# A second spare buffer for up weights, earlier loads of the second quad's gates, and a compact copy of the sample rows, in a one-core hybrid decoder step

## The chip, the cores and the metric

The kernel runs on one core of a Trainium2 chip. The metric is device time in microseconds (us), the median of three runs.

## The reference, cut to what matters

One inference step for 256 prompt tokens and 32 sample tokens (8 sequences of 4) at model width 1024, all in float32. A pooling mixer and a gated linear-attention mixer are merged, multiplied by `w_out` and added to `x`. Then comes a routed mixture of 32 experts, and a last norm:

```python
x = x + einsum(merged, w_out)
h = rmsnorm(x, norm2_w)
# group top-1 of 4, expert top-2 of 8, weights combine[token, expert]
act = silu(h @ w_gate[e]) * (h @ w_up[e]) * combine[..., e]
x = x + sum_e act @ w_down[e]        # w_gate, w_up: 1024 x 256, w_down: 256 x 1024
y = rmsnorm(x, final_norm_w)
```

The weights of one expert are three matrices of 1 MB each, so the mixture reads 96 MB.

## The kernel before, in words

**Stages.** Input projection, mixers, branch products, output product, mixture, final norm. The change touches the output product and the mixture, which fill the span from about 329 us to its end.

**Output product** (PE `wo_half` L1868, DVE `step_evac` L2778). It runs in nine steps, `WO_STEPS`: step 0 makes the 32 sample rows, steps 1 to 4 and 5 to 8 make the two prompt tiles, 256 output columns per step. Step 1 + j and step 5 + j read the j-th buffer of `w_out`. These four buffers are slots 2, 3, 4, 5. The semaphore `wo_pe` counts the finished steps, `wo_dve` the steps that DVE (L2782) has added to `x2`. The sample rows lie in `x2s` with 128 partitions by 256 columns: partition 32 g + token holds columns 256 g onwards. After each step POOL multiplies the new rows by the norm weights (`n2b`, `n2bs`) into `x2p` (prompt, L889) or `x2d` (sample, L881). `x2d` is 128 by 1024, block diagonal: for each chunk k of 128 features it holds a 128 by 128 matrix in which only the four 32 by 32 blocks on the diagonal aren't zero. POOL clears all of it first (L874) and writes the blocks in four linked instructions. ACT scales `x2p` and `x2d` by the row norms (L1207).

**Gather.** `G` holds for each token tile a 128 by 128 matrix of zeros and ones that says which token sits in which of 128 seats: 4 experts (a "quad") times 32 seats. PE gathers the rows of a quad with one product per chunk k and token tile t, `src[:, k, :]` against `G[:, t, :]`, all 128 by 128: in `gathers` (L1927) for the first quad, 8 chunks by 3 tiles, and in `gather_next` (L2019) for each next one, 24 products in a row. A float32 product shows as two matmul records in the trace.

**Quads.** There are 8 quads of 4 experts. For quad q PE runs (`quad_products`, L2092) gate products, up products (L2013, 32 products each, in tiles of 128 by 32), two flips, the gather for quad q + 1 (L2025), the down products (L2068) and `way_back` (L2088, L2085), which spreads the result to the tokens. The last two quads are ordered otherwise (`last_pair`): gate(6), gather, up(6), gate(7), down(6), up(7), down(7).

**Loads.** All weight loads are issued in a fixed order by SP (L582, L591), each 1 MB into one slot; a load waits until the slot's last reader is done, and all that is behind it in the queue waits too. Gates go to slots 8, 9, 11, 12 (`EVEN_GATES`) or 2, 3, 4, 5 (`ODD_GATES`), ups to 13, 14, 15, 6 (`UPS`), downs to 7, 10, 0, 1. SP's order around the change:

1. gates, ups and downs of quad 0;
2. gates of quad 1 into slots 2 to 5, each after `item_read` of the slot's last user, which for a buffer of `w_out` is `wo_pe` >= 9, the end of all steps (L407);
3. after the last logits (`lgt` >= 3) one up weight of quad 1 into a spare slot (`SPARE`, slot 16, in the room of `h2T`);
4. gates of quad 2 in eight half loads (`gates_in_parts` L585), four of them when PE is half through the gate products of quad 0 (`m_gate0`), four after all of them (`m_gate`);
5. the other three ups of quad 1 after `m_up` >= 1;
6. downs of quad 1 after `m_dn1` >= 1, the end of quad 0's down products; gates of quad 3 after `m_gate` >= 2; ups of quad 2 after `m_up` >= 2; downs of quad 2 after `m_dn1` >= 2, and so on.

The final norm's weights are loaded by ACT's queue (L1169, L1171) after quad 1, into the room of `n2b`.

```python
held, v = item_read(reader_ahead(A_ITEMS, s))   # L630
sp.wait_ge(held, v)
part_load(1, w_gate, QE + e, s)
...
sp.wait_ge(S["m_dn1"], q)                       # L610
for e, s in enumerate(DOWNS):
    part_load(q, w_down, first + e, s)
```

Of the kernel before, what the change touches and what calls it, by code (L numbers as in the profile page):

```python
# [12 lines left out]
P = 128  # L13
# [102 lines left out]
SPARE, EARLY = N_SLOTS, UPS[0]  # L116
# [13 lines left out]
def hybrid_step(nc, x_prompt, x_sample, cache_pool, cache_conv, state_delta, norm1_w, w_in, w_pool,  # L130
# [24 lines left out]
    with ExitStack() as ctx:  # L155
# [3 lines left out]
        def sem(name):  # L159
            return ctx.enter_context(nc.semaphore(name))  # L160
# [159 lines left out]
        n2b = b.take(D)  # L320
        n2bs = b.take(D // 4)
        rows_w = b.take(2 * T).rearrange("p (k t) -> p k t", k=2)
        rows_c = b.take(2 * T).rearrange("p (k t) -> p k t", k=2).bitcast(I32)
# [9 lines left out]
        x2d = b.take(D).rearrange("p (k q) -> p k q", k=KD)  # L333
        h2T = b.take(KD * T).rearrange("p (k t) -> p k t", k=KD)
        back1 = b.take(T)
        assert b.at <= b_end, (b.at, b_end)
        slots.append(h2T.rearrange("p k t -> p (k t)")[:, 0:SLOT])
# [56 lines left out]
        ring_in = [sem(f"ring_in{i}") for i in range(N_SLOTS + 1)]  # L394


        def item_read(i):
# [8 lines left out]
            return S["wo_pe"], len(WO_STEPS)  # L406
# [56 lines left out]
        def _(sp):  # L463
# [138 lines left out]
            def ups(q, first):  # L602
                sp.wait_ge(S["m_up"], q)
                for e, s in enumerate(UPS):
                    if s != EARLY or not (isinstance(q, int) and q == 1):
                        part_load(q, w_up, first + e, s)
# [27 lines left out]
            part_load(1, w_up, QE, SPARE)  # L634
# [33 lines left out]
        def _(pool):  # L668
# [205 lines left out]
            link(nc.gpsimd.memset(x2d, 0.0))  # L874
            pool.wait_ge(S["nb_in"], 16 * 5)
            for n, (t, j) in enumerate(WO_STEPS):
                pool.wait_ge(S["wo_dve"], n + 1)
                if t == 2:
                    for g in range(4):
                        own = slice(TS * g, TS * g + TS)  # L880
                        ins = nc.gpsimd.tensor_tensor(x2d[own, :, own], x2s[own, :].rearrange("p (q k) -> p k q", k=KD),  # L881
                                                      n2bs[own, :].rearrange("p (q k) -> p k q", k=KD), ALU.mult)
                        if g < 3:
                            link(ins)
                    ins.then_inc(S["xp_pool"], 1)
                    pool.wait_ge(S["xp_pool"], 1)
# [15 lines left out]
        def _(act):  # L902
# [376 lines left out]
            for i in range(PEEL):  # L1279
                for u in range(2):  # L1280
                    quad_acts(i, u)
                if i == 0:
                    act.wait_ge(S["xp_pool"], len(WO_STEPS))
                    norm_rows(fnb, fnbs, final_norm_w, "nb_in")
# [24 lines left out]
        def _(pe):  # L1309
# [616 lines left out]

            def gathers(t, first=False, last_tile=False):  # L1927

                src = x2d if t == 2 else x2p[:, t]
                for k in range(KD):  # L1930
                    ins = mm(ps[k // 4][:, P * (k % 4):P * (k % 4) + P], src[:, k, :], G[:, t, :],
# [1101 lines left out]
```

## Time and profile before

| what | value |
|---|---|
| median of three runs | 602.62 us (601.82 to 602.76) |
| the profiled execution | 602.27 us |
| its span | 600.5 us |
| PE busy | 548.7 us (91%) |
| PE weight load busy | 409.4 us (68%) |
| DVE, ACT, POOL busy | 45%, 25%, 23% |
| moved by DMA | 158.59 MB, mean 264 GB/s |

The shares are means over stages with different limits: PE's 91% comes from the first 425 us, the DMA engines are full in the last 200. The span is the profiled stretch; the 1.8 us between it and the execution's time lie around it.

### The profile page before, as it was taken

The numbers are of one execution on the slowest core, as the hardware profiler recorded it, in microseconds if no ns is written. First come the engines' busy times: TensorE is split into PE (matmuls) and PEld (weight loads), VectorE is DVE, ScalarE is ACT, GpSimd is POOL, SyncE is SP. The second block draws the span as 40 slices with busy tenths as digits, with TensorE's granted clock in tenths as the row PEclk, the third lists the DMA queues.
The fourth block names the chain that finished last, engine by engine and source line by source line (L and its number), as shares of the span: only waits on it lengthen the run. The fifth ranks groups of instructions, "written<-read, shape, count | busy, mean of one in ns | idle before, by whom it ended". The sixth has DMA issues, their size and how long they took to land.

```text
span 600.5 us, 12000 instructions
## 1 busy us (share of the span) xinstructions
PE 548.7 (91%) x4820; PEld 409.4 (68%) x4820; DVE 270.1 (45%) x754; ACT 147.2 (25%) x389; POOL 135.2 (23%) x228
## 2 busy tenths in 40 slices
PE   8999999999999999999999999999495959699873
PEld 7899999777877755578889888755262626266431
DVE  4567767755443426146546244651314040414125
ACT  3366465237720002033100133111010101010012
POOL 5777774121200540035004421200000000000000
PEclk9999999999999999999999999999789898999988
DMA  9755444839934273542378944999999999999982
GB/s 242 232 159 151 154 142 141 281 112 332 306 87 134 45 264 110 172 123 89 109 260 350 381 180 199 365 422 420 409 422 419 423 420 419 422 420 419 421 330 79
DMA packets 82582, 158.59 MB, mean 264 GB/s; under 512 B 11245, under 2 KB 65274, under 8 KB 70849
## 3 DMA queue, kind: packets, MB, share of 16 engines
q1 hardware_dynamic: 79724, 154.22, 70.1%
q10 hardware_dynamic: 2805, 3.62, 2.0%
q8 instruction: 38, 0.62, 0.4%
q14 instruction: 15, 0.12, 0.1%
HBM read 150.05 MB, written 7.96 MB: 263 GB/s over the span
## 4 chain that ended last, share of the span: by engine, by line
PE 72%; DMA 23%; DVE 2%; SPq 1%; issue 1%; ACT 1%; DVEq 0%; ACTq 0%
DMA arena<-in_w_up_dram 21%; PE ps L1360 21%; PE ps L1369 13%; PE ps L2013 8%; PE ps L1881 5%; PE ps L1830 3%; PE ps L1784 3%; PE ps L1313 2%; DMA arena<-in_w_in_dram 1%; SPq L582 1%; PE ps L1823 1%; PE ps L2088 1%; PE ps L2068 1%; PE ps L1566 1%; PE ps L1530 1%; PE ps L2025 1%
## 5 line engine op out<-in xcount | busy, mean ns | idle before, releaser
L1360 PE MATMUL ps<-arena 128*128 128x288 f32 x480 | 130.1, 416 | 1.2 <-DMA arena<-in_w_in_dram 1.2
L1360 PEld LDWEIGHTS ps<-arena 128*128 128x128 f32 x480 | 87.3, 190 | 26.8 <-issue 3.1
L2013 PE MATMUL ps<-arena 128*32 128x256 f32 x1024 | 69.3, 433 | 29.0 <-DMA arena<-in_w_up_dram 27.6
L2013 PEld LDWEIGHTS ps<-arena 128*32 128x32 f32 x1024 | 40.1, 124 | 56.7 <-issue 43.2
L1369 PE MATMUL ps<-arena 128*128 128x144 f32 x616 | 78.3, 288 | 0.0
L1369 PEld LDWEIGHTS ps<-arena 128*128 128x128 f32 x616 | 76.3, 190 | 2.5 <-issue 1.9
L2229 DVE SCALAR_TENSOR_TENSOR ps<-arena,ps 128x312 f32<-128x312 f32 x72 | 39.1, 545 | 2.4 <-ACT ps L1021 0.9
L2025 PE MATMUL ps<-arena 128*128 128x128 f32 x336 | 38.7, 276 | 0.0
L2025 PEld LDWEIGHTS ps<-arena 128*128 128x128 f32 x336 | 38.1, 192 | 0.4 <-DVE arena L2898 0.4
L2919 DVE TENSOR_TENSOR arena<-arena,ps 128x256 f32<-128x256 f32 x8 | 3.4, 421 | 66.8 <-issue 36.6
L2088 PE MATMUL ps<-arena 128*128 128x512 f32 x64 | 31.2, 618 | 1.9 <-ACT arena L1258 1.0
L1313 PE MATMUL ps<-arena 128*128 128x128 f32 (+7 forms) x162 | 26.5, 282 | 5.8 <-DVE arena L2919 4.7
L1881 PE MATMUL ps<-arena 128*128 128x256 f32 x128 | 31.0, 385 | 0.0
L2068 PE MATMUL ps<-arena 128*32 128x512 f32 x256 | 29.3, 596 | 1.7 <-DMA arena<-in_w_down_dram 1.2
L2935 DVE TENSOR_TENSOR arena<-arena,ps 128x512 f32<-128x512 f32 (+1 forms) x40 | 24.7, 633 | 13.7 <-PE ps L2088 13.7
L1313 PEld LDWEIGHTS ps<-arena 128*128 128x128 f32 (+7 forms) x162 | 19.0, 148 | 12.7 <-issue 5.6
L2088 PEld LDWEIGHTS ps<-arena 128*128 128x128 f32 x64 | 10.3, 189 | 23.0 <-issue 13.8
L2926 DVE COPY arena<-ps 128x512 f32<-128x512 f32 x8 | 5.5, 692 | 44.4 <-PE ps L2068 44.4
L1881 PEld LDWEIGHTS ps<-arena 128*128 128x128 f32 x128 | 23.1, 190 | 2.9 <-issue 0.4
L1252 ACT ACTIVATE arena<-ps 128x256 f32<-128x256 f32 x8 | 3.1, 383 | 82.0 <-PE ps L1313 82.0
L1830 PE MATMUL ps<-arena 128*128 128x144 f32 x168 | 21.0, 287 | 0.1
L1830 PEld LDWEIGHTS ps<-arena 128*128 128x128 f32 x168 | 20.8, 190 | 0.4 <-DVE arena L2741 0.3
(410 smaller groups left out, 747.3 us busy)
## 6 DMA issues: line engine op xcount, KB each, us to landing
arena<-in_w_up_dram SPq DMA_DIRECT2D x32, 1024.0 KB, 17.3
arena<-in_w_gate_dram SPq DMA_DIRECT2D x28, 1024.0 KB, 18.1
arena<-in_w_down_dram SPq DMA_DIRECT2D x28, 1024.0 KB, 18.6
arena<-in_w_in_dram SPq DMA_DIRECT2D x26, 1024.0 KB, 6.7
out_dram<-arena SPq DMA_DIRECT2D x9, 512.0 KB, 7.6
arena<-in_w_branch_delta_dram SPq DMA_DIRECT2D x4, 1024.0 KB, 6.3
arena<-in_w_out_dram SPq DMA_DIRECT2D x4, 1024.0 KB, 5.4
arena<-in_w_gate_dram SPq DMA_DIRECT2D x8, 512.0 KB, 9.5
```

What stands on the lines that cost most here:

```text
L1313: return nc.tensor.transpose(out, in_, ident[0:m, 0:m])
L1360: last = mm(ps[n % 2][:, 0:T], w[:, k, P * (n % 2):P * (n % 2) + P], hT[:, k, :], start=(k == 0), stop=(k == KD - 1))
L1369: last = mm(to[:, 0:HT], left[:, k, :], right[:, k, :], start=(first and k == 0), stop=(k == HK - 1), skip_group_check=True)
L1784: last = mm(ps[BP_BANK[d]][:, 0:T], w[:, k, P * (d % 4):P * (d % 4) + P], ypT[:, k, :], start=(k == 0), stop=(k == NG - 1))
L1830: last = mm(bank[:, 0:HT], left[:, k, :], right[:, k, :], start=(first and k == 0), stop=(k == HK - 1), skip_group_check=True)
L1881: last = mm(bank[:, 0:256], merged[:, k, P * t:P * t + P], w[:, k, :], start=(k == 0), stop=(k == KD - 1))
L2013: last = mm(to[CAP * e:CAP * e + CAP, 0:FE], xgT[u][:, k, CAP * e:CAP * e + CAP], w[e][:, k, :], start=(k == 0), stop=(k == KD - 1))
L2025: last = mm(ps[k // 4][:, P * (k % 4):P * (k % 4) + P], src[:, k, :], G[:, t, :], start=(t == ORDER[0]), stop=(t == ORDER[-1]))
L2068: last = mm(ps[5 + half][CAP * e:CAP * e + CAP, :], actT[u][:, c, CAP * e:CAP * e + CAP], w[:, c, 512 * half:512 * half + 512], start=(c = ...
L2088: last = mm(bank[:, :], back[:, P * t:P * t + P], dn[:, 512 * half:512 * half + 512], start=True, stop=True)
L2229: ins = V.scalar_tensor_tensor(c, e[:, j:j + NACC], smallT[:, NQKV * j + n:NQKV * j + n + 1], c, ALU.mult, ALU.add)
L2935: V.tensor_tensor(v, v, bank[:, 0:v.shape[1]], ALU.add).then_inc(S["m_yadd"], 1)
```

## The change

- `item_read` lets the j-th buffer of `w_out` go at `wo_pe` >= 6 + j, its own last step, in place of 9 for all.
- A second spare slot (17, `spare2`) takes a second up weight of quad 1. It lies where `n2b` and `n2bs` are, so SP waits for `xp_pool` >= 9, POOL's last product, before it loads there. Slot 14 joins slot 13 in `EARLY`: no load goes to it for quad 1. Both spares share a semaphore, on which PE waits for 32.
- ACT waits for `m_up` >= 2 before it loads the final norm's weights into `n2b`.
- To make room, `x2d` shrinks from 1024 to 256 columns: 128 partitions by 8 chunks by 32. The clearing of it is gone, and POOL writes it in one instruction. The four row copies `rows_c`, `rows_w` go to four separate rooms.
- The gather product of the sample tile becomes four products for each chunk, each 32 rows by 32 columns of stationary data (`src[own, k, :]`) against 32 rows by 128 of `G`, into its own 32 partitions of the bank. `gather_next` takes the tiles in the order 0, 2, 1 (before: 2, 0, 1).

```diff
@@ -113,7 +113,7 @@
 UPS, DOWNS = (13, 14, 15, 6), (7, 10, 0, 1)
 LAST_DOWNS = EVEN_GATES
 N_SLOTS = 16
-SPARE, EARLY = N_SLOTS, UPS[0]
+SPARES, EARLY = (N_SLOTS, N_SLOTS + 1), UPS[0:2]
 
 
 WO_STEPS = [(2, None)] + [(t, j) for t in range(2) for j in range(WO_ITEMS)]
@@ -317,10 +317,10 @@
         x2 = b.take(2 * D).rearrange("p (n d) -> p n d", n=2)
         x2s = b.take(D // 4)
         slots.append(b.take(SLOT))
-        n2b = b.take(D)
-        n2bs = b.take(D // 4)
-        rows_w = b.take(2 * T).rearrange("p (k t) -> p k t", k=2)
-        rows_c = b.take(2 * T).rearrange("p (k t) -> p k t", k=2).bitcast(I32)
+        spare2 = b.take(SLOT)
+        n2b = spare2[:, 0:D]
+        n2bs = spare2[:, D:D + D // 4]
+        row_rooms = [b.take(T)]
         assert b.at <= qk_at + NQKV * T
         fnb, fnbs = n2b, n2bs
         b = Cut(qk_at + NQKV * T)
@@ -330,11 +330,15 @@
         assert b.at <= work0 and len(slots) == N_SLOTS
         b = Cut(work0)
         x2p = b.take(2 * D).rearrange("p (n k q) -> p n k q", n=2, k=KD)
-        x2d = b.take(D).rearrange("p (k q) -> p k q", k=KD)
+        x2d = b.take(D // 4).rearrange("p (k q) -> p k q", k=KD)
+        row_rooms += [b.take(T), b.take(T)]
         h2T = b.take(KD * T).rearrange("p (k t) -> p k t", k=KD)
+        row_rooms.append(arena[:, b.at - KD * T + SLOT:b.at - KD * T + SLOT + T])
+        b.take(max(0, SLOT + T - KD * T))
         back1 = b.take(T)
         assert b.at <= b_end, (b.at, b_end)
-        slots.append(h2T.rearrange("p k t -> p (k t)")[:, 0:SLOT])
+        rows_c, rows_w = [v.bitcast(I32) for v in row_rooms[0:2]], row_rooms[2:4]
+        slots.extend((h2T.rearrange("p k t -> p (k t)")[:, 0:SLOT], spare2))
         b = Cut(b_end)
         xgT_room = b.take(2 * KD * P)
         xgT = [xgT_room[:, KD * P * j:KD * P * (j + 1)].rearrange("p (k t) -> p k t", k=KD) for j in range(2)]
@@ -392,6 +396,7 @@
 
         S = Sems()
         ring_in = [sem(f"ring_in{i}") for i in range(N_SLOTS + 1)]
+        ring_in.append(ring_in[SPARES[0]])
 
 
         def item_read(i):
@@ -403,7 +408,7 @@
             i -= BP_ITEMS
             if i < BD_ITEMS:
                 return S["bd_pe"], delta_product(i, P4) if i in BD_FAST else 2
-            return S["wo_pe"], len(WO_STEPS)
+            return S["wo_pe"], len(WO_STEPS) - WO_ITEMS + i - BD_ITEMS + 1
 
 
         free = [0] * N_PROJ
@@ -602,7 +607,7 @@
             def ups(q, first):
                 sp.wait_ge(S["m_up"], q)
                 for e, s in enumerate(UPS):
-                    if s != EARLY or not (isinstance(q, int) and q == 1):
+                    if s not in EARLY or not (isinstance(q, int) and q == 1):
                         part_load(q, w_up, first + e, s)
 
             def ups_downs(q, first):
@@ -631,7 +636,9 @@
                 sp.wait_ge(held, v)
                 part_load(1, w_gate, QE + e, s)
             sp.wait_ge(S["lgt"], NT)
-            part_load(1, w_up, QE, SPARE)
+            part_load(1, w_up, QE, SPARES[0])
+            sp.wait_ge(S["xp_pool"], len(WO_STEPS))
+            part_load(1, w_up, QE + 1, SPARES[1])
 
             def pair_loads(i, ahead):
                 first, then = (i % (QUADS // 2)) * (2 * QE), (ahead % (QUADS // 2)) * (2 * QE)
@@ -871,19 +878,12 @@
             sum_delta_weights(2)
             pool.wait_ge(S["y_done"], N_Y)
             sum_delta_weights(3)
-            link(nc.gpsimd.memset(x2d, 0.0))
             pool.wait_ge(S["nb_in"], 16 * 5)
             for n, (t, j) in enumerate(WO_STEPS):
                 pool.wait_ge(S["wo_dve"], n + 1)
                 if t == 2:
-                    for g in range(4):
-                        own = slice(TS * g, TS * g + TS)
-                        ins = nc.gpsimd.tensor_tensor(x2d[own, :, own], x2s[own, :].rearrange("p (q k) -> p k q", k=KD),
-                                                      n2bs[own, :].rearrange("p (q k) -> p k q", k=KD), ALU.mult)
-                        if g < 3:
-                            link(ins)
-                    ins.then_inc(S["xp_pool"], 1)
-                    pool.wait_ge(S["xp_pool"], 1)
+                    nc.gpsimd.tensor_tensor(x2d, x2s.rearrange("p (q k) -> p k q", k=KD),
+                                            n2bs.rearrange("p (q k) -> p k q", k=KD), ALU.mult).then_inc(S["xp_pool"], 1)
                 else:
                     cols = slice(256 * j, 256 * j + 256)
                     nc.gpsimd.tensor_tensor(x2p[:, t, :, TS * j:TS * j + TS], x2[:, t, cols].rearrange("p (q k) -> p k q", k=KD),
@@ -1281,6 +1281,7 @@
                     quad_acts(i, u)
                 if i == 0:
                     act.wait_ge(S["xp_pool"], len(WO_STEPS))
+                    act.wait_ge(S["m_up"], 2)
                     norm_rows(fnb, fnbs, final_norm_w, "nb_in")
             act.wait_ge(S["route"], 1)
             end = act.value_load(more_i[0:1, 0:1], min_val=0, max_val=MORE_MAX) + QUADS // 2
@@ -1924,12 +1925,16 @@
                         last = mm(bank[at:at + m, 0:NE], strU[0:m, 0:m], picks[0:m, t, :], start=(not before), stop=True)
                     last.then_inc(S["ranked"], 1)
 
+            def tile_rows(t):
+                return [slice(TS * g, TS * g + TS) for g in range(4)] if t == 2 else [slice(0, P)]
+
             def gathers(t, first=False, last_tile=False):
 
                 src = x2d if t == 2 else x2p[:, t]
                 for k in range(KD):
-                    ins = mm(ps[k // 4][:, P * (k % 4):P * (k % 4) + P], src[:, k, :], G[:, t, :],
-                             start=(first and k % 4 == 0), stop=(last_tile and k % 4 == 3), skip_group_check=True)
+                    for own in tile_rows(t):
+                        ins = mm(ps[k // 4][own, P * (k % 4):P * (k % 4) + P], src[own, k, :], G[own, t, :],
+                                 start=(first and k % 4 == 0), stop=(last_tile and k % 4 == 3), skip_group_check=True)
                     if last_tile and k % 4 == 3:
                         ins.then_inc(S[f"m_g{k // 4}"], 1)
 
@@ -1995,10 +2000,10 @@
                 n = i + 1 if table in (EVEN_GATES, ODD_GATES) else 2 * i + u + 1
                 for s in table:
                     base = loads_in(s) if s < RA else 0
-                    if s == SPARE:
-                        pe.wait_ge(ring_in[s], 16)
+                    if s in SPARES:
+                        pe.wait_ge(ring_in[s], 16 * len(SPARES))
                         continue
-                    if s == EARLY and not (isinstance(n, int) and n == 1):
+                    if s in EARLY and not (isinstance(n, int) and n == 1):
                         base = -1
                     if s in EVEN_GATES and not (isinstance(n, int) and n == 1):
                         base = 1
@@ -2020,10 +2025,11 @@
 
                 pe.wait_ge(S["m_G"], q + (NT + 1))
                 for k in range(KD):
-                    for t in ORDER:
+                    for t in (0, 2, 1):
                         src = x2d if t == 2 else x2p[:, t]
-                        last = mm(ps[k // 4][:, P * (k % 4):P * (k % 4) + P], src[:, k, :], G[:, t, :],
-                                  start=(t == ORDER[0]), stop=(t == ORDER[-1]))
+                        for own in tile_rows(t):
+                            last = mm(ps[k // 4][own, P * (k % 4):P * (k % 4) + P], src[own, k, :], G[own, t, :],
+                                      start=(t == 0), stop=(t == 1), skip_group_check=True)
                     if k % 4 == 3:
                         last.then_inc(S[f"m_g{k // 4}"], 1)
 
@@ -2048,7 +2054,7 @@
 
                 q = 2 * i + u
                 wait_from(S["m_act"], q)
-                ups = (SPARE,) + UPS[1:] if isinstance(q, int) and q == 1 else UPS
+                ups = SPARES + UPS[2:] if isinstance(q, int) and q == 1 else UPS
                 loaded(ups, i, u)
                 products(i, u, ups, ps[3]).then_inc(S["m_up"], 1)
...
```

## Rows read from the trace of the kernel before

**Rows 1.** The page: GB/s by slice of 15 us; the chain by line
```profile
GB/s 242 232 159 151 154 142 141 281 112 332 306 87 134 45 264 110 172 123 89 109 260 350 381 180 199 365 422 420 409 422 419 423 420 419 422 420 419 421 330 79
...
DMA arena<-in_w_up_dram 21%; PE ps L1360 21%; PE ps L1369 13%; PE ps L2013 8%; PE ps L1881 5%; PE ps L1830 3%; PE ps L1784 3%; PE ps L1313 2%; DMA arena<-in_w_in_dram 1%; SPq L582 1%; PE ps L1823 1%; PE ps L2088 1%; PE ps L2068 1%; PE ps L1566 1%; PE ps L1530 1%; PE ps L2025 1%
```

**Rows 2.** SP's waits: us, times, longest us
```profile
SPq L582 <- PE ps L1881: 32.5, 1, 32.5
```

**Rows 3.** Timeline of SP's queue, 366 to 409 us
```profile
366.74 1.97 SPq L582 DMA_DIRECT2D arena<-in_w_gate_dram  x4
368.92 0.33 SPq L582 DMA_DIRECT2D arena<-in_w_up_dram  x1
378.51 5.17 SPq L591 DMA_DIRECT2D arena<-in_w_gate_dram  x8
383.73 2.06 SPq L582 DMA_DIRECT2D arena<-in_w_up_dram  x3
396.89 1.75 SPq L582 DMA_DIRECT2D arena<-in_w_down_dram  x4
404.73 1.75 SPq L582 DMA_DIRECT2D arena<-in_w_gate_dram  x4
408.18 1.75 SPq L582 DMA_DIRECT2D arena<-in_w_up_dram  x4
```

**Rows 4.** Busy time by stretch; at the end PEclk, DMA share, GB/s
```profile
354.00:366.00 12.00, 12.00 (x65) 10.62 (x65) 5.18 (x25) 3.81 (x11) 3.34 (x3) 1.00 0.00 0
366.00:378.50 12.50, 11.64 (x113) 9.92 (x115) 8.14 (x38) 5.33 (x9) 2.43 (x6) 1.00 0.86 344
366.00:400.00 34.00, 33.14 (x315) 23.85 (x314) 18.23 (x57) 7.30 (x13) 4.80 (x13) 1.00 0.95 369
402.00:580.00 178.00, 143.63 (x1472) 83.32 (x1464) 49.20 (x118) 12.15 (x25) 0.00 (x0) 0.91 1.01 418
```

**Rows 5.** Timeline of DVE, 353 us
```profile
353.77 0.42 DVE L2782 SCALAR_TENSOR_TENSOR arena<-ps,arena 128x256 f32<-128x256 f32 x1 [1.20 <-PE ps L1881]
```

**Rows 6.** Timeline of POOL, 333 us
```profile
333.13 4.66 POOL L881 TENSOR_TENSOR arena<-arena 32x256 f32<-32x256 f32 x4 [11.60 <-DVE arena L2782]
```

**Rows 7.** Timeline of PE, 366 to 375 and 384 to 402 us
```profile
368.72 2.03 PE L1931 MATMUL ps<-arena 128*128 128x128 f32 x16
371.30 0.41 PE L1924 MATMUL ps<-late_room 128*128 128x32 f32 x2 [0.55 <-DVE late_room L2817]
...
387.74 5.52 PE L2025 MATMUL ps<-arena 128*128 128x128 f32 x48
393.19 3.64 PE L2068 MATMUL ps<-arena 128*32 128x512 f32 x32
```

**Rows 8.** Chain of waits: start us, us, what
```profile
106.26 3.88 PE ps L1360 x16
...
159.32 3.63 PE ps L1566 x128
```

**Rows 9.** Timeline of PE around one L1554 insertion, 190 to 196 us
```profile
190.74 0.75 PE L1360 MATMUL ps<-arena 128*128 128x288 f32 x2
...
194.81 0.64 PE L1554 MATMUL ps<-arena 32*32 32x128 f32 x16
195.38 0.51 PE L1360 MATMUL ps<-arena 128*128 128x288 f32 x1
```

**Rows 10.** Timeline of PE and SP, the last two quads
```profile
547.86 5.63 PE L2025 MATMUL ps<-arena 128*128 128x128 f32 x48
...
554.34 3.66 PE L2013 MATMUL ps<-arena 128*32 128x256 f32 x64 [0.86 <-DMA arena<-in_w_up_dram]
...
558.28 1.90 SPq L582 DMA_DIRECT2D arena<-in_w_up_dram  x4
...
574.52 5.35 PE L2013 MATMUL ps<-arena 128*32 128x256 f32 x64 [2.21 <-DMA arena<-in_w_up_dram]
```

**Rows 11.** Busy time by stretch: the last up products
```profile
575.00:578.50 3.50, 3.50 (x41) 2.23 (x37) 0.00 (x0) 0.00 (x0) 0.00 (x0) 0.54 1.06 390
```

More of the change, by code:

```diff
@@ L2901, in way_back @@
             def way_back(turns):
-                V.scalar_tensor_tensor(back, rows_c[:, 0, :], place[:, 0:1], rows_w[:, 0, :], ALU.is_equal, ALU.mult).then_inc(S["turns"], 1)
-                V.scalar_tensor_tensor(back1, rows_c[:, 1, :], place[:, 0:1], rows_w[:, 1, :], ALU.is_equal, ALU.mult).then_inc(S["turns"], 1)
+                V.scalar_tensor_tensor(back, rows_c[0], place[:, 0:1], rows_w[0], ALU.is_equal, ALU.mult).then_inc(S["turns"], 1)
+                V.scalar_tensor_tensor(back1, rows_c[1], place[:, 0:1], rows_w[1], ALU.is_equal, ALU.mult).then_inc(S["turns"], 1)
                 dve.wait_ge(S["turns"], turns + 2)
@@ L2942, in quad_acts @@
                         dve.wait_ge(S["rows_pe"], k + 1)
-                        V.tensor_copy((rows_c if k < 2 else rows_w)[:, k % 2, :], ps[ROW_BANK[k]][:, 0:T]).then_inc(S["rows_ev"], 1)
+                        V.tensor_copy((rows_c if k < 2 else rows_w)[k % 2], ps[ROW_BANK[k]][:, 0:T]).then_inc(S["rows_ev"], 1)
                     dve.wait_ge(S["rows_ev"], 4)
```

## The prediction

> **What bounds the kernel now.** I read the page first, then SP's waits, then stretches of the DMA engines. In every slice from 390 to 570 us the DMA engines move 409 to 423 GB/s, and the chain that ended last runs for 21% of the span through up loads [rows 1]. From 402 to 580 us the mean is 418 GB/s at a DMA share of 1.01 [rows 4]: the mixture's weights come as fast as they can, one load of 1 MiB (1.049 MB) each 2.51 us. So the end is set by when that unbroken stream begins and by how much it has to carry.
>
> Before it there is a hole. SP waits 32.5 us for the end of the output product [rows 2], and from 354 to 366 us nothing is moved [rows 4]. The change fills this hole with the four gates of quad 1, and adds a load behind them. The question is whether work put into the hole shortens the stream, or only opens a second hole later. For that the order of SP's issues is to be read [rows 3]: four gates at 366.74, one up at 368.92, eight half loads of gates from 378.51, three ups from 383.73, four downs from 396.89. That is 12 MiB, 12.58 MB, ahead of the downs. From 366 to 400 us the engines move 34 us x 369 GB/s = 12.55 MB [rows 4]. So the twelve loads are through at 400.1 us, and the downs, issued 3.2 us earlier, find the engines still busy. The stream has no gap at 396.89, but the queue is only 3.2 us deep there.
>
> **The hole after the change.** The loads of quad 1's gates wait for steps 6, 7, 8 and 9. DVE's addition of the sixth step begins at 353.77 [rows 5], so the first goes then and the last at 366.74 as before; both spares follow at about 369 us. These loads are through by 366.74 + 1.5 + 3 x 2.51 = 375.8 us. (The 1.5 us are the start of an idle queue: from 366 to 378.5 us the engines move 12.5 x 344 = 4.30 MB [rows 4], which is 10.3 us of work at 418 GB/s, so it began in effect at 368.2.) Then the engines stand idle until the half loads at 378.51. Behind those come only two ups in place of three: 6 MiB, 15.1 us from 380.0, through at 395.1. Half loads ran slower before, which the mean of 369 holds; if two more microseconds go there it is 397. In either case the queue is empty when the downs are issued, and their issue waits for PE to finish the down products of quad 0. That semaphore, not the buffers, becomes the bound. If it comes at the same time, the downs start to flow at 396.89 + 1.5 = 398.4 in place of 400.1. **The most that the earlier loads and the spare can give is therefore 1.7 us**, not the 2.5 us of a load, nor the ten of four. What is late next is PE.
>
> **Did PE get slower before that semaphore?** The chain from 372 us is PE nearly without gaps. `gather_next` for quad 1 takes 48 records from 387.74, and the down products start at 393.19, right behind it [rows 7]: 5.45 us, 0.227 us for each full product of two records. Whatever is added to this gather delays the downs by as much. Per chunk the change takes out one full product and puts in four of 32 by 32, eight records, between two full products. The nearest rows for this are the sample tiles L1554: 32 by 32 tiles, 128 columns, each in its own 32 partitions of one bank, sixteen records between full products of L1360. Without them sixteen L1360 records take 3.88 us [rows 8]. With them, the next sixteen start at 190.74, the tiles at 194.81 (4.07 us, 0.19 more), and L1360 goes on at 195.38 (0.57 us) [rows 9]. The insertion costs 0.76 us. Four narrow tiles of 128 columns side by side run at 3.63 us for 128 records [rows 8], 28.4 ns a record, so 0.45 us of it are the records and 0.31 us the way into the narrow tiles and back.
>
> Per chunk then: 8 x 28.4 ns + 0.31 = 0.53 us in place of 0.227, that is +0.31 us, and 8 chunks make **+2.4 us in `gather_next`**. The lower bound is that the switch costs nothing here, 8 x (0.227 - 0.227) = 0. The upper one takes the tiles at the pace inside the insertion, 0.57/16 = 35.6 ns, beside the 0.31 us: 8 x (0.595 - 0.227) = 2.9 us, and 4 us if loads of full weights behind a tile take another 0.13 us a chunk (half of a full product's time, rounded up). I take 2.4, since L1554 is the same shape in the same order.
>
> The Trainium skill says in TensorEngine Tiling (Array Packing), Key Properties, that changing the tiling mode drains TensorE. By that rule a compact tile between full ones isn't free; without the rule one would put this gather at no loss and the change at 1.7 us faster. The trace agrees with the rule, by the 0.31 us worked out above.
>
> **The first gathers.** The sample tile's gather starts at 368.72 and takes 16 records, and PE then waits for DVE until 371.30 [rows 7]. After: 64 x 28.4 ns + 0.31 = 2.1 us, done at 370.9. The cover is 0.4 us; at 35.6 ns a record it would be 371.3, still even. Cost nothing.
>
> **Edits that I cost at nothing.** POOL's four instructions of the sample step, 4.66 us together [rows 6], become one and the clearing goes; PE doesn't wait for POOL there (from 354 to 366 us it is busy 12.00 of 12 us [rows 4]), since DVE's addition and the `w_out` products go on without it, so nothing is won. ACT's scaling of `x2d` shrinks under the same cover. The row copies keep their sizes. SP's wait for `xp_pool` comes no later than the logits' (POOL multiplies while PE makes them), and behind it stand only the half loads of 378.51. ACT's wait for `m_up` >= 2 stands after quad 1's down evacuation, by when it is long met. PE's wait on both spares is at quad 1's ups, after 401 us; both have landed by 378.
>
> **Do the later issues hold?** All after the first gather move by 2.4 us, those after the second by 4.9. Gates of quad 3, 404.73 [rows 3], become 407.2; the downs then flow until 398.4 + 2.4 + 10.0 = 410.8, so 2.1 us of the 3.6 are left after the 1.5 us of a start. Ups of quad 2, 408.18, have a further 10 us. In the last quads the gather of 547.86 ends 2.4 us later, the ups after it start at about 556.2 in place of 554.34, and SP's ups of 558.28 go at 560.1, while the downs ahead of them flow until about 564 [rows 10]. The stream holds.
>
> **Sum.** Earlier loads and spare -1.7, gather +2.4: +0.7 us on the profiled execution's 602.27, so 603.0. That execution lay 0.35 us below the median of the runs, 602.62; I give 603.3 for the median. A measurement of this kernel can tell about 0.2%, 1.2 us, from no change, so this is **no difference**.
>
> **The rivals.**
>
> *The switch hides (faster).* Weight loads of the next tiles run beside the current products and the gather stays at 5.5 us. Then the full 1.7 us come out, 600.9. For it: weight loads lie under products almost everywhere. Against: the insertion's 0.76 us.
>
> *The clock stays up at the end (still no difference).* The last up products run from 574.52 for 5.35 us where the ones at 554.34 took 3.66 [rows 10], at a granted clock of 0.54 of 2.4 GHz, so mostly at 1.2 GHz [rows 11], after a wait of 2.2 us for the load. PE is busier before it after the change, as the gather moves everything behind it. If the clock stays at 2.4 GHz, the tail loses 1.7 us: 601.6.
>
> *The row groups take turns (slower).* At one place, the eight tile records of a chunk, each takes a full record's 0.114 us because the four tiles write one bank: 8 x (0.91 + 0.31 - 0.227) = 7.9 us, less 1.7: 608.8. It decides from a tile record of 60 ns on (8 x (0.48 + 0.31 - 0.227) = 4.5, 605.4). Against: sixteen such records took 0.57 us, not 1.8.
>
> The Trainium skill gives a rule of this kind in TensorEngine Tiling (Array Packing), Gotcha 1: different row tiles can't access the same PSUM bank at once. The trace speaks against it at that same place, L1554.
>
> *The switch costs more than there (slower).* A gather of +4 us, the upper bound above, gives 602.6 + 4.0 - 1.7 = 604.9. From +2.9 us on it could be told from no change.
>
> *The change doesn't do what it says:* an early wait that I think is met, such as `xp_pool`, holds the half loads. It would have to come after 378.51, ten microseconds late. 1 in 100.
>
> **How the numbers follow.** Forecast, gather +1.6 to +3.2 us: 0.5. Switch hidden or nearly: 0.2. Clock stays up: 0.08. Gather +3.2 to +5: 0.16. Turns, wholly or in part: 0.05. The rest 0.01. With a gather of +2.9 and more the time is past 603.8, so 0.08 of the forecast's 0.5 count as slower. Same: 0.42 + 0.07 of the clock's 0.08 = 0.49. Faster: 0.2 + 0.01 = 0.21. Slower: 0.08 + 0.16 + 0.05 + 0.01 = 0.30. The range runs from the hidden switch, 600.9 or 0.2 less, to a gather of +4: 600.7 to 605.0. What is left out is the turns and a part of either end.
>
> **What would show it.** In the profile after: SP issues single gate loads from 353.8 us; a DMA hole from about 376 to 380 us and one from about 396 to 400; the L2025 group at quad 0 with 96 records over 7.9 us; the downs of quad 1 issued at 399.3 with an idle queue, the first landing some 5 us later; 418 GB/s from there. I am wrong on the gather if it takes under 6.5 or over 9 us, and wrong on the stream if a hole comes after 402 us or if the downs still find a busy queue.

## The result and the profile after

The changed kernel takes **605.33 us** (median of 4 runs, 605.16 to 605.61) against 602.34 for the kernel before: ratio 1.0052, 95% interval 1.0033 to 1.0071, 3 us slower. I had forecast 603.3 and no difference, and a range up to 605.0. The profiled execution took 605.44 us, its span is 603.7, PE is busy 563.3 us of it (548.7 before) with 5204 matmul records (4820). The 384 more records are the narrow products: in each of eight gathers, eight chunks with eight narrow records for two full ones.

The page of the changed kernel, part 2, in slices of 15.1 us (before: [rows 1]):

```profile
GB/s 239 233 159 150 153 141 141 280 115 327 282 109 132 56 251 116 164 132 79 115 252 348 403 279 290 282 296 423 407 421 418 421 419 422 421 419 422 348 368 79
```

The slices at 347 and 362 us show the plan of the change: 180 and 199 GB/s before, where the output product ends, and 279 and 290 now. The slice at 377 us has fallen from 365 to 282: the gap between the early loads and the half loads, which was expected. But the slice at 392 us has gone from 422 to 296 and the one at 558 us from 421 to 348: two places where the full stream of before now has a hole.

The timeline of SP's queue in the changed kernel (start us, us, engine line, issue; before: [rows 3]):

```profile
354.57 13.37 SPq L587 DMA_DIRECT2D arena<-in_w_gate_dram  x4
369.79 0.81 SPq L587 DMA_DIRECT2D arena<-in_w_up_dram  x2
379.39 4.50 SPq L596 DMA_DIRECT2D arena<-in_w_gate_dram  x8
384.57 0.80 SPq L587 DMA_DIRECT2D arena<-in_w_up_dram  x2
400.35 2.06 SPq L587 DMA_DIRECT2D arena<-in_w_down_dram  x4
408.19 1.76 SPq L587 DMA_DIRECT2D arena<-in_w_gate_dram  x4
...
565.05 2.03 SPq L587 DMA_DIRECT2D arena<-in_w_up_dram  x4
```

The gates go one by one from 354.57 and both spares at 369.79. The downs of quad 1 go at 400.35, 3.46 us later than before; and the last row, the ups of quad 7, go at 565.05, before at 558.28 [rows 10], 6.77 us later.

Busy time by stretch, changed kernel: after the stretch and its length stand the busy us of PE, PEld, DVE, ACT and POOL with their counts, and at the end PEclk, DMA share and GB/s (before: [rows 4]):

```profile
354.00:366.00 12.00, 12.00 (x67) 10.65 (x66) 5.39 (x25) 3.54 (x11) 3.34 (x3) 1.00 0.64 208
...
376.00:380.00 4.00, 4.00 (x60) 2.77 (x62) 3.66 (x14) 1.88 (x2) 1.95 (x7) 1.00 0.28 111
380.00:396.00 16.00, 16.00 (x200) 11.03 (x196) 7.21 (x16) 0.77 (x2) 1.73 (x6) 1.00 0.94 357
396.00:398.00 2.00, 2.00 (x26) 0.79 (x26) 0.00 (x0) 0.60 (x1) 0.00 (x0) 1.00 0.69 291
398.00:401.50 3.50, 3.50 (x27) 1.16 (x20) 0.81 (x2) 0.60 (x1) 0.00 (x0) 1.00 0.19 26
402.00:563.00 161.00, 140.51 (x1579) 74.37 (x1582) 46.21 (x112) 10.78 (x22) 0.00 (x0) 0.94 1.01 419
563.00:566.50 3.50, 2.52 (x46) 1.27 (x38) 0.42 (x1) 0.38 (x1) 0.00 (x0) 1.00 0.62 185
...
562.00:564.00 2.00, 2.00 (x44) 1.22 (x40) 0.00 (x0) 0.00 (x0) 0.00 (x0) 1.00 0.77 320
564.00:566.00 2.00, 1.20 (x18) 0.40 (x10) 0.42 (x1) 0.00 (x0) 0.00 (x0) 1.00 0.33 139
566.00:568.00 2.00, 1.83 (x36) 1.38 (x40) 0.00 (x0) 0.38 (x1) 0.00 (x0) 1.00 1.00 283
```

The hole of before (354 to 366 us, 0 GB/s) carries 208. The queue runs dry between 396 and 398 us (291 GB/s there), as predicted, and stays so until the downs flow: 26 GB/s from 398 to 401.5. From 402 to 563 us the stream is as full as before, 419. Then from 563 to 566.5 us it is at 185. This second hole I had said would not come.

PE in the changed kernel around both holes (before: [rows 7], [rows 10]), and last the ups of quad 5 in the kernel before:

```profile
369.69 1.95 PE L1936 MATMUL ps<-arena 32*32 32x128 f32 x64
372.18 0.41 PE L1925 MATMUL ps<-late_room 128*128 128x32 f32 x2 [0.53 <-DVE late_room L2823]
...
388.62 8.10 PE L2031 MATMUL ps<-arena 128*128 128x128 f32 x96
396.65 3.64 PE L2074 MATMUL ps<-arena 128*32 128x512 f32 x32
```

```profile
526.98 5.09 PE L2018 MATMUL ps<-arena 128*32 128x256 f32 x64 [6.70 <-DMA arena<-in_w_up_dram]
...
533.02 8.10 PE L2031 MATMUL ps<-arena 128*128 128x128 f32 x96
...
549.38 3.66 PE L2018 MATMUL ps<-arena 128*32 128x256 f32 x64 [0.30 <-issue]
552.97 8.21 PE L2031 MATMUL ps<-arena 128*128 128x128 f32 x96
561.10 3.66 PE L2018 MATMUL ps<-arena 128*32 128x256 f32 x64
...
578.78 3.66 PE L2018 MATMUL ps<-arena 128*32 128x256 f32 x64 [1.12 <-DMA arena<-in_w_up_dram]
```

```profile
524.46 5.14 PE L2013 MATMUL ps<-arena 128*32 128x256 f32 x64 [5.20 <-DMA arena<-in_w_up_dram]
```

The next-quad gather takes 96 records and 8.03 us to the start of the down products (388.62 to 396.65); before it took 5.45. In the second fence PE runs from the ups of quad 5 (526.98) to those of quad 6 (561.10) without waiting for a load once, with two such gathers on the way (533.02 and 552.97). Before, the ups of quad 6 had to wait 0.86 us for their load [rows 10]; now the load waits for PE.

**Where the 3.2 us of span went.** All work before the change's part runs 0.86 us later in this execution (quad 0's ups are issued at 331.10, before at 330.24). I take it for scatter: over the 13 profiles of this study that issue lies between 329.5 and 331.7 us, and the earliest is that of a kernel with the same compact copy (grouped, below). The downs of quad 1 lose 3.46 - 0.86 = 2.6 us. Of these, 1.6 were slack before: there the downs were issued 3.2 us before the queue ran dry at 400.1, and a start takes some 1.6. So the stream starts 1.0 us later. The second hole costs, summed over the three stretches of 2 us from 562 (320, 139 and 283 GB/s in place of 418), 2.45 us. The last up products take 3.66 us in place of 5.35, and the rest of the tail gives 0.6 of that back: -1.1. Together 0.86 + 1.0 + 2.45 - 1.1 = 3.2. Of these the 1.0 and the 2.45 belong to the change.

### The profile page after: what moved, and what is told of

It reads as the page before. It is cut to its first block, busy times and chain, and to the rows that moved or that the text cites. A ratio compares the mean times of both kernels' runs of the same rounds, so it can differ in the third digit from the quotient of the medians.

```text
span 603.7 us, 12766 instructions
## 1 busy us (share of the span) xinstructions
PE 563.3 (93%) x5204; PEld 408.0 (68%) x5204; DVE 269.7 (45%) x754; ACT 146.4 (24%) x389; POOL 131.3 (22%) x224
## 4 chain that ended last, share of the span: by engine, by line
PE 78%; DMA 13%; issue 3%; SPq 3%; DVE 2%; ACT 1%; POOL 0%; DVEq 0%; POOLq 0%
PE ps L1361 20%; PE ps L1370 13%; DMA arena<-in_w_up_dram 11%; PE ps L2018 7%; PE ps L2031 5%; PE ps L1882 5%; PE ps L1831 3%; PE ps L1314 3%; PE ps L1785 3%; PE ps L2094 2%; PE ps L2074 2%; DMA arena<-in_w_down_dram 2%; SPq L662 2%; PE ps L1824 1%; PE ps L1567 1%
## 5 line engine op out<-in xcount | busy, mean ns | idle before, releaser
L1361 PEld LDWEIGHTS ps<-arena 128*128 128x128 f32 x480 | 87.1, 190 | 26.4 <-issue 3.9
L2018 PE MATMUL ps<-arena 128*32 128x256 f32 x1024 | 64.9, 411 | 18.5 <-DMA arena<-in_w_up_dram 17.2
L1370 PEld LDWEIGHTS ps<-arena 128*128 128x128 f32 x616 | 76.3, 190 | 2.4 <-issue 1.9
L2018 PEld LDWEIGHTS ps<-arena 128*32 128x32 f32 x1024 | 37.7, 118 | 44.1 <-issue 29.0
L2031 PE MATMUL ps<-arena 32*32 32x128 f32 (+1 forms) x672 | 56.8, 287 | 0.0
L2031 PEld LDWEIGHTS ps<-arena 32*32 32x32 f32 (+1 forms) x672 | 38.3, 132 | 18.3 <-issue 11.1
L2094 PEld LDWEIGHTS ps<-arena 128*128 128x128 f32 x64 | 10.3, 188 | 23.0 <-issue 13.8
L1882 PEld LDWEIGHTS ps<-arena 128*128 128x128 f32 x128 | 23.1, 190 | 3.0 <-issue 0.4
L1831 PEld LDWEIGHTS ps<-arena 128*128 128x128 f32 x168 | 20.8, 190 | 0.4 <-DVE arena L2747 0.3
L972 ACT ACTIVATE arena<-ps 128x288 f32<-128x288 f32 x16 | 6.5, 409 | 56.9 <-PE ps L1361 56.8
```

What stands on the lines that cost most here:

```text
L1361: last = mm(ps[n % 2][:, 0:T], w[:, k, P * (n % 2):P * (n % 2) + P], hT[:, k, :], start=(k == 0), stop=(k == KD - 1))
L1370: last = mm(to[:, 0:HT], left[:, k, :], right[:, k, :], start=(first and k == 0), stop=(k == HK - 1), skip_group_check=True)
L1831: last = mm(bank[:, 0:HT], left[:, k, :], right[:, k, :], start=(first and k == 0), stop=(k == HK - 1), skip_group_check=True)
L1882: last = mm(bank[:, 0:256], merged[:, k, P * t:P * t + P], w[:, k, :], start=(k == 0), stop=(k == KD - 1))
L2018: last = mm(to[CAP * e:CAP * e + CAP, 0:FE], xgT[u][:, k, CAP * e:CAP * e + CAP], w[e][:, k, :], start=(k == 0), stop=(k == KD - 1))
L2031: last = mm(ps[k // 4][own, P * (k % 4):P * (k % 4) + P], src[own, k, :], G[own, t, :], start=(t == 0), stop=(t == 1), skip_group_check=True)
```

## The experiments

Two theories stood at first. A: the loads do what they should, and the narrow gather products cost it twice, at the stream's start and before the last quad's ups. B: the loads themselves cost it. Ratios are against the kernel before, run beside each set on the same chip.

| run | ratio (95% interval) | median, before beside it |
|---|---|---|
| full_copy | 0.9975 (0.9962 to 0.9988) | 600.44, 602.08 |
| compact_only | 1.0065 (1.0050 to 1.0080) | 605.75, 602.08 |
| gates_early | 0.9995 (0.9980 to 1.0009) | 601.63, 602.08 |
| grouped | 0.9971 (0.9960 to 0.9983) | 600.11, 602.08 |
| narrow_first | 1.0032 (1.0016 to 1.0047) | 604.00, 601.94 |
| narrow_later | 1.0030 (1.0018 to 1.0042) | 603.53, 601.94 |
| spare_only | 0.9984 (0.9973 to 0.9996) | 601.04, 601.94 |
| two_trips | one run | 600.88, 601.94 |
| before_copy | 1.0002 (0.9991 to 1.0013) | 601.74, 601.41 |
| order_only | 1.0005 (0.9993 to 1.0017) | 602.26, 601.41 |
| spare_again | 0.9993 (0.9982 to 1.0004) | 601.24, 601.41 |

**full_copy: the change without the compact copy.** The block diagonal copy stays, with POOL's clearing and its four steps. Room for it is there: in the changed kernel the work area has 559 unused columns at its end and the arena 713. The second takes two of the row copies (576 columns), and with these gone the first takes the 768 columns that `x2d` grows by.

```diff
-        x2d = b.take(D // 4).rearrange("p (k q) -> p k q", k=KD)
-        row_rooms += [b.take(T), b.take(T)]
+        x2d = b.take(D).rearrange("p (k q) -> p k q", k=KD)
+        row_rooms += [high.take(T), high.take(T)]
...
-                return [slice(TS * g, TS * g + TS) for g in range(4)] if t == 2 else [slice(0, P)]
+                return [slice(0, P)]
```

> All of the change but the compact copy: the sample rows' copy stays block diagonal (1024 columns, cleared and written in four steps as before), and all gather products are 128 by 128. Theory A (the narrow tiles cost it all: 2.5 us more in the first next-quad gather, and a second stall of the load stream before the last quad's ups): gather 5.5 us, downs of quad 1 issued some 2.5 us earlier than in the changed kernel relative to the end of the output product, no hole near 564 us; about 1.7 us faster than before, 600.7. Theory B (the loss comes from the loads: gates loaded beside the output product, or the second spare): it stays slower than before, 603 to 605.

Measured 1.6 us faster than before. Timeline of PE, then of SP:

```profile
387.15 5.52 PE L2038 MATMUL ps<-arena 128*128 128x128 f32 x48
...
552.83 3.66 PE L2025 MATMUL ps<-arena 128*32 128x256 f32 x64 [1.01 <-DMA arena<-in_w_up_dram]
```

```profile
396.30 2.01 SPq L587 DMA_DIRECT2D arena<-in_w_down_dram  x4
...
556.77 1.90 SPq L587 DMA_DIRECT2D arena<-in_w_up_dram  x4
```

Against the changed kernel the gather is 2.6 us shorter, the downs of quad 1 go at 396.30, the ups of quad 6 wait for their load again (1.01 us), and those of quad 7 are issued at 556.77, no hole behind them. Theory B falls: with all the new loads and waits in place the kernel is faster than before. Some of the 1.6 us may not be the stream's: see the controls below.

**compact_only: the kernel before with the compact copy and its gather products.** The diff is the changed kernel's in `gathers`, `gather_next` and POOL's sample step; `x2d` keeps its old room, and all loads are as before.

> The kernel before with the compact copy and its narrow gather products alone; all loads as before. Theory A: the stream starts 0.8 us later than before and has a hole of 2 to 3 us before the last quad's ups, so about as slow as the changed kernel, 605 to 606. Theory B: the compact copy costs under 1 us, so at most 603.3.

Measured 1.0065, as slow as the changed kernel: its interval and that of 1.0052 overlap. Timeline of PE, then busy time by stretch (last columns PEclk, DMA share, GB/s):

```profile
389.21 8.10 PE L2023 MATMUL ps<-arena 128*128 128x128 f32 x96
...
562.82 3.66 PE L2010 MATMUL ps<-arena 128*32 128x256 f32 x64
```

```profile
400.00:402.00 2.00, 2.00 (x15) 0.68 (x4) 0.72 (x2) 0.00 (x0) 0.00 (x0) 1.00 0.88 295
402.00:404.00 2.00, 2.00 (x5) 0.60 (x4) 1.47 (x3) 0.00 (x0) 0.00 (x0) 1.00 0.73 283
...
564.00:566.00 2.00, 2.00 (x44) 1.23 (x40) 0.00 (x0) 0.00 (x0) 0.00 (x0) 1.00 0.49 205
566.00:568.00 2.00, 1.03 (x18) 0.34 (x10) 0.42 (x1) 0.27 (x1) 0.00 (x0) 1.00 0.54 119
```

Both holes are there without any new load: here the queue of 12 MiB runs dry at 400 to 404 us (295 and 283 GB/s in place of 418: 1.2 us), and again from 564 to 568. So the first hole costs about the same with the new loads (1.0 us) and without them: once the slow gather holds the downs' issue back, the earlier loads and the spare bring next to nothing, and what the change was made for is lost.

**gates_early: the release of the four buffers alone.**

```diff
-            return S["wo_pe"], len(WO_STEPS)
+            return S["wo_pe"], len(WO_STEPS) - WO_ITEMS + i - BD_ITEMS + 1
```

> The kernel before with the earlier release of the output weights' buffers alone. Theory A: 17 MiB are still ahead of the downs of quad 1, but five of them have gone before the half loads, so the queue is empty at about 399.5 us in place of 400.1: 0 to 0.6 us faster, 602.0. Theory B: slower by a good part of the 3 us.

Measured 0.9995, no difference, though the interval leaves room for a gain of up to 1.2 us. Busy time by stretch:

```profile
396.00:398.00 2.00, 2.00 (x12) 0.68 (x4) 1.07 (x2) 0.00 (x0) 0.00 (x0) 1.00 1.01 426
398.00:400.00 2.00, 2.00 (x6) 0.59 (x4) 1.47 (x3) 0.00 (x0) 0.00 (x0) 1.00 1.00 406
```

From the half loads at 378.21 on, 7 MiB lie ahead of the downs. They begin at 379.7 after an idle stretch, need 17.6 us at full pace and more at that of half loads, so they end between 397.3 and 399.5. The downs, issued at 396.59, can flow from 398.1. There is no hole, and little was won: the ups of quad 6 start at 554.75, before at 554.34. The stream itself did move. Adding up GB/s by stretches of 1 us gives the time from SP's issue of quad 0's ups to the point where 40 MB are left to move: 158.7 us here, 159.8, 159.5 and 159.6 in the three kernels with all loads as before and full products (before, before_copy, order_only). In this execution the 0.9 us didn't reach the last ups, which begin at 574.62, before at 574.52; why isn't known.

**grouped: the changed kernel with all narrow products of a gather in a row.**

```diff
-                for k in range(KD):
-                    for t in (0, 2, 1):
-                        src = x2d if t == 2 else x2p[:, t]
+                for t in (0, 2, 1):
+                    src = x2d if t == 2 else x2p[:, t]
+                    for k in range(KD):
```

with `start` at the first chunk of each bank and `stop` at its last.

> The changed kernel with the next-quad gathers in another order: tile 0 for all 8 chunks, then the 64 narrow records in a row, then tile 1. One way into the narrow mode and back in place of eight. Theory A, with 0.31 us for each way in and back and 28 ns for a record: gather 5.45 + 0.3 = 5.8 us, and the two halves of the result are ready later but nothing on PE waits for that; no hole at the end; 1.3 us faster than before, 601.0. Rival A2 (the narrow records themselves are slow, not the switch): gather stays near 8 us and the time near 605.

Measured 0.9971: the fastest, with full_copy. Timeline of PE, and below it the same of two_trips, where the narrow products of four chunks stand in a row:

```profile
387.04 5.81 PE L2031 MATMUL ps<-arena 128*128 128x128 f32 x96
...
572.95 3.66 PE L2018 MATMUL ps<-arena 128*32 128x256 f32 x64 [1.94 <-DMA arena<-in_w_up_dram]
```

> The changed kernel with the narrow products of four chunks in a row, so two ways into the narrow mode and back in each next-quad gather. Theory A: grouped took 5.81 us with one way, the changed kernel 8.1 with eight; 0.32 us for each makes 6.1 us with two. Time near grouped, 600.5. Rival A2 (it was the order of the tiles, not the number of switches): near 5.8 or near 8.

```profile
388.10 6.13 PE L2032 MATMUL ps<-arena 128*128 128x128 f32 x96
```

The same 96 records take 5.81 us with one way into the narrow tiles and back, 6.13 with two and 8.10 with eight: 0.32 and 0.33 us for each further one. Taking 32 full records of 0.114 us (3.63 us) and one switch off 5.8 leaves 1.86 us for 64 narrow ones, 29 ns each. So the narrow records are as cheap as they should be and A2 falls; the switches are the price. What takes the time in a switch isn't shown: no run tells whether the engine empties itself there or waits for a load of weights that no product covers.

**narrow_first and narrow_later: narrow products by chunk in chosen gathers.** Both are full_copy, with the narrow products reading the diagonal blocks of the full copy.

```diff
+                narrow = isinstance(q, int) and q == 0          # narrow_later: not (...)
                 for k in range(KD):
                     for t in (0, 2, 1):
...
+                        parts = [slice(TS * g, TS * g + TS) for g in range(4)] if t == 2 and narrow else [slice(0, P)]
```

> All of the change with the block diagonal copy (as in full_copy, which ran 1.65 us faster than before), but narrow products, chunk by chunk, in the first next-quad gather alone; they read the diagonal blocks of that copy. Theory A (two losses, each with its place): only the start of the stream is hit, by 2.5 us against full_copy: 0.9 us slower than before, 603.0, and no hole before the last quad's ups. Rival A3 (the stream takes up a late start, only the end counts): as full_copy, 600.4.

> The same with narrow products in all next-quad gathers but the first. Theory A: the stream starts as early as in full_copy, and the last quads come too late for it: PE takes 34.1 us from quad 5's ups to quad 6's ups, as in the changed kernel, so the last quad's ups are issued about 38 us after quad 5's ups began, some 2 us after the engines run dry: 2 to 3 us slower than full_copy, 602.5 to 603.4. Rival A3: 603 or more, as the whole loss of the changed kernel would sit there (605).

Measured 1.0032 and 1.0030. narrow_first, timeline of PE and busy time by stretch:

```profile
388.26 8.10 PE L2040 MATMUL ps<-arena 128*128 128x128 f32 x96
...
412.12 5.52 PE L2040 MATMUL ps<-arena 128*128 128x128 f32 x48
...
556.35 3.66 PE L2025 MATMUL ps<-arena 128*32 128x256 f32 x64 [1.32 <-DMA arena<-in_w_up_dram]
```

```profile
398.00:400.00 2.00, 2.00 (x21) 0.54 (x14) 0.00 (x1) 0.60 (x1) 0.00 (x0) 1.00 0.07 29
...
564.00:566.00 2.00, 1.12 (x23) 0.47 (x12) 0.00 (x0) 0.38 (x1) 0.00 (x0) 1.00 1.04 434
```

narrow_later, the same:

```profile
387.30 5.52 PE L2040 MATMUL ps<-arena 128*128 128x128 f32 x48
...
549.70 8.21 PE L2040 MATMUL ps<-arena 128*128 128x128 f32 x96
557.84 3.66 PE L2025 MATMUL ps<-arena 128*32 128x256 f32 x64
```

```profile
398.00:400.00 2.00, 2.00 (x5) 0.59 (x4) 1.47 (x3) 0.00 (x0) 0.00 (x0) 1.00 0.86 352
562.00:564.00 2.00, 1.53 (x23) 1.03 (x27) 0.14 (x1) 0.38 (x1) 0.00 (x0) 1.00 0.60 156
```

With the first gather narrow there is the first hole (29 GB/s at 398 us) and none at the end (434 at 564 us), and the ups of quad 6 wait for their load. With the later ones narrow the stream starts early (352 GB/s at 398 us) and has the hole at the end (156 at 562 us), where the ups of quad 6 wait for nothing. In the profiles they are 3.6 and 2.6 us longer than full_copy (601.3 and 600.3 against 597.7); corrected by where quad 0's ups are issued (330.75 and 329.79 against 329.65) that is 2.5 us each. Each place costs by itself, and both together make the changed kernel in about this size: 603.7 - 597.7 = 6.0, less 1.45 of the same correction, 4.55. A3 falls with narrow_first, which it put at 600.4. The medians say the same less neatly. They are 3.7 and 3.2 us over full_copy (each against before beside it), known to about 1 us each, and each is slower than was expected (604.00 for 603.0, and 603.53 for 602.5 to 603.4); together they are more than the changed kernel's 4.6. So that each place costs is shown, and how exactly the parts make the whole is not.

**spare_only: full_copy with the gates released as before, twice.**

> full_copy with the gates of quad 1 released as before, so the second spare alone. Theory A: 12 MiB are again issued between 366.7 us and the downs of quad 1, at 418 GB/s from 368.2, so they are through at the same 400 us as before and the spare gives nothing: within 0.5 us of before. Rival (each part gives its share by itself): 1.2 us faster, since the gates alone gave 0.3.

> spare_only once more. Theory A says no gain from the spare alone, so with a second set of runs the ratio should come nearer to 1 than 0.9984. If the 0.9 us are real it stays at 0.9984.

Measured 0.9984 and 0.9993. Theory A expected nothing; the first interval excludes 1, the second doesn't. At the places of the theory next to nothing has moved: SP issues the downs at 396.95 and the last ups at 558.76, and both profiles hold 406 GB/s or more at 398 us. By the count to 40 MB left they are at 159.2 and 159.2 us, 0.3 to 0.6 ahead of the three kernels above. What differs between the two is the length of the last up products (timeline of PE, spare_only and spare_again):

```profile
574.74 3.66 PE L2025 MATMUL ps<-arena 128*32 128x256 f32 x64 [1.96 <-DMA arena<-in_w_up_dram]
```

```profile
574.17 5.35 PE L2025 MATMUL ps<-arena 128*32 128x256 f32 x64 [1.89 <-DMA arena<-in_w_up_dram]
```

**before_copy and order_only: controls.** The first is the kernel before unchanged, the second has only the tile order 0, 2, 1 with full products.

> The kernel before once more, unchanged, as a control for the 0.9 us by which spare_only came out faster. If that is the scatter of this measurement, the ratio here may lie as far from 1 (0.998 to 1.002), and the last up products, 5.35 us in the profile of before at half the clock and 3.66 us in spare_only, may come out as either in this profile. If before always pays the low clock at the end, they take 5.35 us here too.

> The kernel before with the tiles of the next-quad gather in the order 0, 2, 1, all products full. Nothing is added or removed: gather 5.5 us, same time as before within 0.2%. A rival for the 0.9 us of spare_only: the order itself, which would show here as 601.1.

Measured 1.0002 and 1.0005. Timeline of PE, before_copy:

```profile
575.12 3.66 PE L2013 MATMUL ps<-arena 128*32 128x256 f32 x64 [1.97 <-DMA arena<-in_w_up_dram]
```

The kernel before shows 5.35 us in one profile and 3.66 in another, and spare_only shows both too. So one kernel can have either, and it is worth about 1 us of span. The order of the tiles costs nothing.

How often it comes seems to depend on the kernel. The mean granted clock of the whole execution is 0.967 to 0.971 in the four profiles with 5.35 us and 0.972 or more in the nine with 3.66, and this mean is on record for every run. By this mark 37 of 84 runs of the kernel before had the low clock at the end, and none of the 21 of full_copy and grouped. In the three sets of the kernel before the runs with the mark are slower by 1.1 to 1.5 us in the median, and those beside full_copy without it have a median of 601.45. So of full_copy's 1.6 us about 0.6 would go with the clock at the end and 1.0 with the stream. This is an estimate: the mark was compared in 13 profiles only, and a run can have spent its low clock elsewhere. The spare alone had the mark in 3 of 24 runs, and against the runs of before without it, it gives 0.1 us both times.

## Why the prediction was wrong, point by point

- **The bound and the first hole: right.** The stream, the queue running dry at 396 to 397 us, and PE's down products as what is late next came as written.
- **The most that the loads can give, 1.7 us: right as a bound, and its nearness is in part luck.** full_copy gives 1.6, but by the estimate above some 0.6 of it go with the clock at the end. The stream moved as it says: the count to 40 MB left is 158.0 us in full_copy and 159.5 to 159.8 in the kernels with loads as before, 1.5 to 1.8 us. The gates alone give nothing that could be told (0.9995) and the spare alone little or nothing; whether the two together give more than their sum is open. In the sum the text books the full 1.7 beside the slow gather, where they bring next to nothing, by compact_only. The result for the first place is the same, since the queue's slack of before was as large.
- **The gather, +2.4 us from eight switches at 0.31: right.** It measured +2.6, 8.03 us where the text says 7.9 (the 28.4 ns of a record were read at L1566, whose tiles are 128 by 32; at 32 by 32 it came to 29). Grouped and two_trips give 0.32 for a switch and 29 ns for a record.
- **The edits at nothing: right**, the first gathers too: they end at 369.69 + 1.95 = 371.64, and PE waits another 0.53 us for DVE as before.
- **"Do the later issues hold?": this step failed.** It says of the last quads that the gather of 547.86 "ends 2.4 us later, the ups after it start at about 556.2", and concludes "The stream holds." The gather was left at its old start, though a few lines earlier the text lets the delay grow from 2.4 to 4.9 us. But between the ups of quad 5, which wait for their load, and the ups of quad 6, PE has no wait for a load, and that stretch holds two gathers. Both are on the path: 561.10 - 526.98 = 34.1 us, before 554.34 - 524.46 = 29.9 us with 0.86 us of waiting in it. That is 5.1 us of work more; 0.9 went into the wait, and the rest came out on the issue of quad 7's ups. It went 6.77 us later than before, 1.86 of them with the whole stream, so 4.9 us later against the stream (4.2 from this stretch, 0.7 since the ups of quad 5 began that much later). The text's delay of 1.8 us left it some 2 us of room. In the kernel before there were about 2.2: by the bytes moved, all loads ahead of those ups were through at about 562 us there, not at 564, and 1.6 us go for the start. 4.9 - 2.2 = 2.7, and the second hole measures 2.45. The sign that the text had named for this, a hole after 402 us, came.
- **The sum**: 0.7 us from the first place was nearly right (1.0 in the profile), but the later gathers stood in it at nothing and cost 2.5 at the second place. So 602.3 + 1.0 + 2.5 = 605.8 with the tail as in the profile of before. With the range's upper end at a costlier gather, and not at a second hole, 605.33 lay 0.3 us outside.
- **The rivals**: "the switch hides" fell with 8.03 us; "the row groups take turns" with the 29 ns of a record; "the clock stays up at the end" did occur in this execution, as in 9 of the 13 profiles, and the tail was 1.1 us shorter for it, not 1.7. It came without the change too, but less often there (see the controls). For the changed kernel itself that isn't settled: it has four runs, and its mean clock is higher already before the tail (0.94 from 402 to 563 us, 0.91 from 402 to 580 before [rows 4]). The rule of the Trainium skill, TensorEngine Tiling (Array Packing), Key Properties, that a change of tiling mode drains TensorE agrees with all gather lengths here, at 0.31 to 0.33 us for a way in and back. The rule of the Trainium skill, same page, Gotcha 1, on row tiles and one PSUM bank doesn't show: four row groups wrote one bank at 29 ns a record, where the 128 by 32 tiles of L1566 took 28.4.

## What to carry to other kernels

When an engine that feeds a full transfer stream gets slower per round, follow it from its last real wait, and add the extra of every round between there and the issue that the stream needs; slack that is checked at one place, with the rest left where it was, is not slack. Put small tiles in a row: what a narrow product costs is the way into the mode and back, so one group for each gather saved 2.3 of 2.6 us with no other edit. And run a bundle's parts apart and together: the loads alone gain, the layout edit that made room for them costs more, and the bundle hides both.

The versions that beat both kernels are grouped (600.11 us) and full_copy (600.44), 2.0 and 1.6 us under the kernel before and 5.0 and 4.6 under the changed one, each against the kernel before beside it.

## What the runs showed of the hardware that I had not expected

- The price of going into 32 by 32 tiles and back was the same between products of 128 columns (0.32 us) as between those of 288 in the kernel before (0.31): it didn't grow or shrink with what stood around it.
- The last up products ran at 5.35 us in 4 of 13 profiles (before, gates_early, order_only, spare_again) and at 3.66 in 9, kernels alike included, at a granted clock of 0.57 to 0.60 of 2.4 GHz from 575 to 579 us against 1.00 (in the kernel before 0.50, so 1.2 GHz, from 576 to 578). PE had waited 1.9 to 2.2 us for the load just before them in the four, and 1.0 to 2.0 us in the nine, so the wait alone doesn't decide it; what does is open.
- An idle load queue needed about 1.6 us from SP's issue to full pace again (issued 400.35, 41 GB/s from 400 to 402 us, 381 in the next 2; issued 565.05, 147 GB/s from 566 to 567 us, 418 in the next). So here an issue had to come that much before the queue ran dry; what it came later than that was the hole.
